# Attention's queries and keys computed channel by token, their rotation and the keys' parts made on GpSimd

## The chip, the cores and the metric

The kernel runs on one core of one Trainium2 chip. The metric is device time of that core in microseconds (us), the median of several runs. A core has TensorE (PE, matrix products and transposes, results in PSUM), VectorE (DVE), ScalarE (ACT), GpSimd (POOL) and SyncE (SP, here the queue that issues most DMAs). Each engine runs its own instructions in the order of the program; semaphores make one wait for another.

## What is computed

One layer of a hybrid block on 512 tokens of width 1024 (in float32). The parts that the change touches are the queries and keys of the attention and the gates of the recurrent branch:

```python
h = rmsnorm(x, norm_g[l])
(a_q, a_k, a_v, a_z, i_q, i_k, i_w,
 b_q, b_k, b_v, b_z, b_o, b_i, b_f, g_a, g_b) = jnp.split(h @ w_in[l], offsets, axis=-1)
q_a = partial_rope(a_q.reshape(Bsz, S, A_HEADS, A_HEAD_DIM), pos)     # 8 heads of 64
k_a = partial_rope(a_k.reshape(Bsz, S, A_HEADS, A_HEAD_DIM), pos)
...
# partial_rope: of 64 channels of a head, 16 are rotated by the token's angle, 48 stay
out = jnp.concatenate([x1 * cos - x2 * sin, x1 * sin + x2 * cos, rest], axis=-1)
...
logits = jnp.einsum('bthd,btjhd->bthj', q_b, k_g) * (Dh ** -0.5)      # per head, chosen keys only
...
# recurrent branch (4 heads of 128): P from running sums and maxima of log_f and log_i
num = w_inter * (qc @ C) + (s_qk @ vc)
```

An indexer (i_q, i_k, i_w) gives each token a score for each earlier key; the best 128 keys take part in its softmax. Both branches are gated, projected, summed, projected once more (w_out), added to x and normalised.

## The kernel before

**Three products for one.** Weights and activations are split into a leading part in fp32r (`w_hi`, `h_hi`) and the remainder (`w_lo`, `h_lo`); the helper `three` (L1483) makes hi·hi, hi·lo and lo·hi, L1486 to L1488. The weights of `w_in` come in slots of 128x1024 (L671): SP loads a slot to `w_raw`, ACT rounds it to `w_hi` (`round_slot`, L875), and POOL subtracts to get `w_lo` (`remainder`, L529). A slot's place is free again when PE has used the slot seven before it.

**Units and places.** PE's work in the first half is a list of units: `small`, then for the groups iq0, iq1 (indexer queries, three units each), aq, ak, bq, bk, bv, av, bo, bz, az four units each. A unit is 24 matmuls of 128x512 into one of two banks `pj`, in four quarters of 6; a quarter is a *place*, and `plan` (L112) puts the small side jobs (transposes, scores, attention heads) behind places by numbers written out by hand. Every engine walks the same list of places and does its part of the side jobs there, in order. With `first["ak"]` as 0, the places of ak are 0 to 15, of bq 16 to 31, of bk 32 to 47, of bv (the recurrent branch's values) 48 to 63, of av (attention's values) 64 to 79. A slot of the next group is rounded, and its remainder made, at the start of each unit, for the last unit of a group at its second place.

**Queries and keys before.** The units aq and ak give token rows (128 tokens x 512 channels). ACT copies the bank to `stage` (L992), DVE rotates 16 channels of each head there (L1138 to L1141, `rotated`), PE transposes the four 128x128 blocks (`stage_chan`, L1541) into a bank `tr`; ACT copies the queries to `q_a` (L904), or rounds the keys to `k_parts` (L913), and DVE subtracts for the keys' remainders (L1259). The indexer's queries go the same way and stay so.

**The recurrent branch at the start of av.** For head h, ACT makes `decay` (L932) and `e_row`, POOL cuts the triangle (`decay_b`, L775, at place 4h of av less 2), PE transposes and multiplies (`kt_b`, `qk_b`, place 4h of av), DVE makes `sp` (L1268, waits for the cut), `q_e` (L1271, both inputs in SBUF), two rounds of the top-k search, and `state` (L1289, L1291), and PE's `pv_b` (L1583, L1586, place 4h+4) waits for `sp`, `q_e` and `state`. POOL's `decay_b` of head 0 stands in its queue behind the remainder of av's fourth slot.

**Gates.** `gate_l` holds 8 columns per token; `gate_rows` (L1529) transposes them in two jobs of four transposes, DVE makes the running rows `a_row` and `nm_row` (L1187 to L1197), and `gate_cols` (L1535) turns these back in eight transposes.

## Time and profile before

| | us |
|---|---|
| median of 3 runs | 505.19 (505.15 to 505.41) |
| the profiled execution | 505.35 |
| its span from first to last instruction | 503.6 |
| PE busy | 494.5 (98%) |
| DVE busy | 261.4 (52%) |
| ACT busy | 239.2 (47%) |
| POOL busy | 213.0 (42%) |

The profile is of one execution. Its page gives busy time by engine, the span in 40 slices, the chain of work that ended last, and groups of instructions; the trace behind it gives each instruction's start and length, and what its engine was waiting for just before. Matmuls are pipelined: a 128x512 matmul is listed with 0.39 us, but the next starts 0.23 us after it, and start to start is what a matmul costs.

### The profile page before, as it was taken

What the parts mean: (1) busy time and instruction counts of PE and PEld (TensorE: products, weight loads), DVE (VectorE), ACT (ScalarE), POOL (GpSimd) and SP (SyncE); (2) the same over time, 40 slices, a digit from 0 to 9 for tenths busy, and PEclk for the clock granted to TensorE, in tenths of its full rate; (3) what the DMA queues carried; (4) which work ended last, traced back from release to release, by engine and by line L of the source; (5) the groups of instructions that cost most, each with busy time, mean ns of one, the idle gap of its engine ahead of it and who ended that gap; (6) DMA issues with size and microseconds to landing.
All of it is one profiled execution on the core that took longest, in us unless ns stands there. A gap on an engine that the chain in (4) does not pass through costs nothing.

```text
span 503.6 us, 6823 instructions
## 1 busy us (share of the span) xinstructions
PE 494.5 (98%) x2518; PEld 411.6 (82%) x2518; DVE 261.4 (52%) x575; ACT 239.2 (47%) x434; POOL 213.0 (42%) x130
## 2 busy tenths in 40 slices
PE   8999999999999999999999999999999999999995
PEld 7688888888888888888788888888888888887885
DVE  3865777877899936525655567531111011125433
ACT  6757655555554455536568652413330333152322
POOL 0675131333344444247487451246534663373000
PEclk9999999999999999999999999999999999999999
DMA  8654432212343243112223112043234426453111
GB/s 284 188 153 128 126 87 79 84 48 80 83 111 99 85 117 104 52 43 85 57 70 85 43 43 65 20 125 104 62 87 125 126 58 193 126 149 144 42 55 72
DMA packets 44841, 48.94 MB, mean 97 GB/s; under 512 B 4996, under 2 KB 30212, under 8 KB 44808
## 3 DMA queue, kind: packets, MB, share of 16 engines
q1 hardware_dynamic: 43944, 47.65, 32.3%
q10 hardware_dynamic: 864, 0.86, 0.5%
q8 instruction: 20, 0.33, 0.3%
q14 instruction: 13, 0.11, 0.1%
HBM read 46.40 MB, written 2.11 MB: 96 GB/s over the span
## 4 chain that ended last, share of the span: by engine, by line
PE 94%; DMA 2%; SPq 1%; POOL 1%; ACT 1%; DVE 1%; issue 1%; DVEq 0%
PE pj L1486 24%; PE pj L1487 24%; PE pj L1488 24%; DMA w_raw<-in_w_in 2%; PE ob L1617 2%; PE tr L1606 2%; PE qb L1554 2%; PE qb L1553 2%; PE ob L1487 1%; PE qb L1487 1%; PE ob L1488 1%; PE qb L1488 1%; PE ob L1486 1%; PE qb L1486 1%; PE tr L1541 1%; PE qb L1601 1%
## 5 line engine op out<-in xcount | busy, mean ns | idle before, releaser
L529 POOL TENSOR_TENSOR w_lo<-w_raw,w_hi 128x1024 fp32r<-128x1024 f32 x70 | 168.9, 2424 | 156.3 <-ACT w_hi L875 156.0
L1486 PE MATMUL pj<-w_hi,h_hi 128*128 128x512 f32 x272 | 109.6, 403 | 0.0
L1488 PE MATMUL pj<-w_hi,h_lo 128*128 128x512 f32 x272 | 106.5, 392 | 0.0
L1487 PE MATMUL pj<-w_lo,h_hi 128*128 128x512 f32 x272 | 106.4, 391 | 0.0
L1486 PE MATMUL pj<-h_hi,w_hi 128*128 128x512 f32 (+1 forms) x200 | 78.1, 390 | 1.0 <-DVE h_lo L1129 1.0
L875 ACT ACTIVATE w_hi<-w_raw 128x1024 fp32r<-128x1024 f32 (+1 forms) x72 | 73.5, 1045 | 9.8 <-DMA w_raw<-in_w_out 6.3
L1488 PE MATMUL pj<-h_hi,w_lo 128*128 128x512 f32 (+1 forms) x200 | 77.9, 389 | 0.0
L1487 PE MATMUL pj<-h_lo,w_hi 128*128 128x512 f32 (+1 forms) x200 | 77.8, 389 | 0.0
L1488 PEld LDWEIGHTS pj<-w_hi,h_lo 128*128 128x128 f32 x272 | 51.1, 188 | 11.4
L1486 PEld LDWEIGHTS pj<-w_hi,h_hi 128*128 128x128 f32 x272 | 51.2, 188 | 8.3 <-issue 0.2
L1487 PEld LDWEIGHTS pj<-w_lo,h_hi 128*128 128x128 f32 x272 | 51.3, 188 | 8.0
L1443 DVE TENSOR_TENSOR prod<-qb,sig 128x512 f32<-128x512 f32 x8 | 5.5, 690 | 77.2 <-PE qb L1488 77.2
L1486 PEld LDWEIGHTS pj<-h_hi,w_hi 128*128 128x128 f32 (+1 forms) x200 | 37.3, 186 | 9.4 <-issue 1.3
L1488 PEld LDWEIGHTS pj<-h_hi,w_lo 128*128 128x128 f32 (+1 forms) x200 | 37.3, 186 | 8.1
L1487 PEld LDWEIGHTS pj<-h_lo,w_hi 128*128 128x128 f32 (+1 forms) x200 | 37.3, 186 | 7.8
L840 POOL TENSOR_TENSOR m_lo<-prod,m_hi 128x512 fp32r<-128x512 f32 x8 | 10.6, 1330 | 60.5 <-ACT m_hi L1088 60.5
L1211 DVE SCALAR_TENSOR_TENSOR score<-ob,idx_w,score 128x512 f32<-128x512 f32 (+2 forms) x45 | 27.7, 616 | 11.5 <-ACT ob L921 8.8
L921 ACT ACTIVATE ob<-qb 128x512 f32<-128x512 f32 (+2 forms) x48 | 22.0, 476 | 16.7 <-PE qb L1554 11.7
L966 ACT ACTIVATE probs<-probs,neg_max 128x128 f32<-128x128 f32 (+3 forms) x32 | 18.0, 562 | 23.3 <-DVE neg_max L1306 23.1
L1088 ACT ACTIVATE m_hi<-prod 128x512 fp32r<-128x512 f32 x8 | 5.1, 632 | 47.3 <-DVE prod L1446 47.3
L1315 DVE COPY probs_t<-tr 128x128 f32<-128x128 f32 (+3 forms) x32 | 15.6, 489 | 22.6 <-PE tr L1606 22.6
L1223 DVE MAX8 top<-score 128x8 f32<-128x512 f32 (+2 forms) x48 | 26.7, 556 | 0.9
(216 smaller groups left out, 817.3 us busy)
## 6 DMA issues: line engine op xcount, KB each, us to landing
w_raw<-in_w_in SPq DMA_DIRECT2D x60, 512.0 KB, 3.6
w_raw<-in_w_out SPq DMA_DIRECT2D x5, 512.0 KB, 3.5
x_tok<-in_x SPq DMA_DIRECT2D x4, 512.0 KB, 5.3
w_raw<-in_w_branch_a SPq DMA_DIRECT2D x8, 256.0 KB, 2.9
w_raw<-in_w_branch_b SPq DMA_DIRECT2D x8, 256.0 KB, 3.3
x_again<-in_x SPq DMA_DIRECT2D x1, 2048.0 KB, 9.3
w_late<-in_w_out SPq DMA_DIRECT2D x3, 512.0 KB, 6.1
out<-y_norm SPq DMA_DIRECT2D x4, 320.0 KB, 2.3
```

The lines of the kernel that those rows point to most:

```text
L529: eng.tensor_tensor(lo[:, 0:m], raw_slot(n)[:, 0:m], hi[:, 0:m].bitcast(F32), ALU.subtract).then_inc(lo_by_dve if n in DVE_SLOTS else lo_b ...
L840: pool.tensor_tensor(m_lo[:, c, :], prod[:, c % 2, 0, :], m_hi[:, c, :].bitcast(F32), ALU.subtract)\
L875: act.activation(split_slot(n)[0][:, 0:m], raw_slot(n)[:, 0:m], ACT.Copy).then_inc(hi_made, 1)
L921: act.activation(ob[s % RELUS][:, 0:w], bank_of(job)[:, 0:w], ACT.Relu, scale=float(IDX_DIM) ** -0.5).then_inc(relu_made, 1)
L966: act.activation(probs[:, s % 2, 0:w], probs[:, s % 2, 0:w], ACT.Exp, scale=-1.0, bias=neg_max[:, s:s + 1], accum_out=p_sum[:, s:s + 1])\
L1211: ins = dve.scalar_tensor_tensor(out=acc, in0=ob[s % RELUS][:, 0:w], scalar=wt, in1=acc, op0=ALU.mult, op1=ALU.add)
L1223: link(dve.max(top8[:, i, :], acc))
L1315: dve.tensor_copy(probs_t[:, s % QUAD, 0:w], bank_of(job)[:, 0:w]).then_inc(probs_t_made, 1)
L1486: pe.matmul(bank, a_hi, b_hi, start=first, stop=False)
L1487: pe.matmul(bank, a_hi, b_lo, start=False, stop=False)
L1488: return pe.matmul(bank, a_lo, b_hi, start=False, stop=last)
L1553: pe.matmul(bank[:, 0:w], queries, ik_hi[:, 0:w], start=True, stop=False)
```

## The change

The units aq and ak are computed channel by token, as bq and bk are: the weights' columns give the rows of the result, so a unit is a block of 128 channels (two heads) over all 512 tokens, and no transpose follows. Rotation now runs across partitions: tables `cos_t` and `sin_t` (made once, from columns that ride in the gates' transpose) hold a factor for each channel row and token; four small DMAs from ACT's queue bring each group's partner rows (8 partitions x 4 x 512 each) into `swapped`, whose other rows are zero; DVE writes result x cos straight from the bank; POOL multiplies `swapped` by `sin_t` and adds it (job `turn`, m 0 to 3 the queries' blocks, 4 to 7 the keys'). The keys' leading parts are made by ACT and their remainders by POOL (job `parts`), in the group bv. The gates' transposes are joined: one `gate_rows` of four transposes 128x128, one `gate_cols` of four 64x64.

```diff
+TURNED = ("aq", "ak")
-STAGED = [u for u in UNITS if u[0] in ("iq0", "iq1", "aq", "ak")]
+STAGED = [u for u in UNITS if u[0] in ("iq0", "iq1")]
+TURNS = [(g, b) for g in TURNED for b in range(KW)]
...
+    for k in range(4):
+        put(first["ak"] + k, "swap", k)
+        put(first["ak"] + 30 + k, "swap", KW + k)
+    for m, p in enumerate((6, 12, 18, 24, 40, 45, 50, 55)):
+        put(first["ak"] + p, "turn", m)
+    for b, p in enumerate((48, 51, 55, 59)):
+        put(first["ak"] + p, "parts", b)
...
+        raw_chan = [at("q_raw", [P, KW, SEQ], F32, z_g2), at("k_raw", [P, KW, SEQ], F32, z_a)]
+        k_chan = at("k_chan", [P, KW, SEQ], F32, z_g2)
...
+            pool.memset(gate_l[:, :, :], 0.0)
+            pool.memset(two_rows[:, :], 0.0)
+            pool.memset(cos_t[:, :], 1.0)
+            pool.memset(sin_t[:, :], 0.0)
+            pool.memset(swapped[:, :, :], 0.0).then_inc(blank_made, 1)
...
+                    if job[0] == "turn":
+                        m = job[1]
+                        g, b = TURNS[m]
+                        pool.wait_ge(rope_made, 4)
+                        pool.wait_ge(swap_in, 64 * (TURNED.index(g) + 1))
+                        pool.tensor_tensor(swapped[:, b, :], swapped[:, b, :], sin_t[:, :], ALU.mult).then_inc(sin_made, 1)
+                        pool.wait_ge(sin_made, m + 1)
+                        pool.wait_ge(cos_made, m + 1)
+                        part = swapped[:, b, :].rearrange("p (t n) -> p t n", n=P)
+                        pool.tensor_tensor(turned_rows(g, b), turned_rows(g, b), part, ALU.add).then_inc(turned, 1)
+                    if job[0] == "parts":
+                        b = job[1]
...
+                        for e in range(2):
+                            src, hi, lo = k_part(b, e)
+                            pool.wait_ge(k_hi_made, 2 * b + e + 1)
+                            pool.tensor_tensor(lo, src, hi.bitcast(F32), ALU.subtract).then_inc(k_lo_made, 1)
+                            pool.wait_ge(k_lo_made, 2 * b + e + 1)
...
+                elif kind == "gate_rows":
...
+                    for first, dst in ((64, cos_t), (96, sin_t)):
+                        for rows in (slice(0, ROT), slice(A_DIM, A_DIM + ROT)):
+                            act.activation(dst[rows, :], bank_of(job)[first:first + ROT, :], ACT.Copy)\
+                                .then_inc(rope_made, 1)
+                elif kind == "swap":
...
+                    act.dma_start(swapped[to:to + HALF, :, :], raw_chan[n][src:src + HALF, :, :]).then_inc(swap_in, 16)
+                elif kind == "parts":
...
+                    act.wait_ge(turned, KW + b + 1)
+                    for e in range(2):
+                        src, hi, _ = k_part(b, e)
+                        act.activation(hi, src, ACT.Copy).then_inc(k_hi_made, 1)
...
-                elif g in ("iq0", "iq1", "aq", "ak"):
+                elif g in TURNED:
+                    act.activation(raw_chan[TURNED.index(g)][:, j, :], src[:, :], ACT.Copy).then_inc(done, 1)
...
+                if g in TURNED:
+                    if g == "ak" and j == 0:
+                        dve.wait_ge(swap_in, 64)
...
+                    dve.tensor_tensor(turned_rows(g, j), pj[u % 2][:, :].rearrange("p (t n) -> p t n", n=P),
+                                      cos_t[:, :].rearrange("p (t n) -> p t n", n=P), ALU.mult).then_inc(cos_made, 1)
...
-                    c = job[1] * B_HEADS
                     for j in range(TILES):
-                        ins = pe.transpose(bank[0:B_HEADS, j * P:(j + 1) * P], gate_l[:, j, c:c + B_HEADS], ident[:, :])
+                        ins = pe.transpose(bank[:, j * P:(j + 1) * P], gate_l[:, j, :], ident[:, :])
...
-                        if g in CHAN_GROUPS:
+                        if g in CHAN_GROUPS + TURNED:
                             a, b = w_part(n, c + j * P, c + (j + 1) * P), h_part(k, 0, SEQ)
```

The numbers of the lines move: `remainder` is L552 in the changed kernel, the decay's cut L826, `sp` L1341, `q_e` L1344, `state` L1362 and L1364, the three products L1567 to L1569.

On PE, at the third place of ak's third unit, before:

```order
444 L1486 MATMUL pj<-w_hi,h_hi 128x512
445 L1487 MATMUL pj<-w_lo,h_hi 128x512
446 L1488 MATMUL pj<-w_hi,h_lo 128x512
447 L1486 MATMUL pj<-w_hi,h_hi 128x512
448 L1487 MATMUL pj<-w_lo,h_hi 128x512
449 L1488 MATMUL pj<-w_hi,h_lo 128x512
450 L1541 MATMUL tr<-ident,stage 128x128 x4
451 L1553 MATMUL qb<-ik_hi,iq_parts 128x256
452 L1554 MATMUL qb<-ik_lo,iq_parts 128x256
```

And the same place after:

```order
441 L1567 MATMUL pj<-h_hi,w_hi 128x512
442 L1568 MATMUL pj<-h_lo,w_hi 128x512
443 L1569 MATMUL pj<-h_hi,w_lo 128x512
444 L1631 MATMUL qb<-ik_hi,iq_parts 128x256
445 L1632 MATMUL qb<-ik_lo,iq_parts 128x256
```

Four transposes are gone, the two operands of each product have changed sides, and the six matmuls of the place and the indexer's score stay as they are. This is so at all eight units of aq and ak.

On POOL, from the top-k part of the program (`v_b`'s ones) to the second cut of `decay`, before:

```order
16 L823 MEMSET v_b 128x16
17 L529 TENSOR_TENSOR w_lo<-w_raw,w_hi 128x1024 x11
18 L775 AFFINE_SELECT decay<-decay 128x512
19 L529 TENSOR_TENSOR w_lo<-w_raw,w_hi 128x1024
20 L775 AFFINE_SELECT decay<-decay 128x512
```

And after, from the last w_lo of bv's slots (the second w_lo of row 38 is av's first slot, rows 43, 47 and 49 its second, third and fourth):

```order
38 L552 TENSOR_TENSOR w_lo<-w_raw,w_hi 128x1024 x2
39 L819 TENSOR_TENSOR k_parts<-k_chan,k_parts 64x512 x2
40 L806 TENSOR_TENSOR swapped<-swapped,sin_t 128x512
41 L810 TENSOR_TENSOR k_chan<-k_chan,swapped 128x512
42 L819 TENSOR_TENSOR k_parts<-k_chan,k_parts 64x512 x2
43 L552 TENSOR_TENSOR w_lo<-w_raw,w_hi 128x1024
44 L806 TENSOR_TENSOR swapped<-swapped,sin_t 128x512
45 L810 TENSOR_TENSOR k_chan<-k_chan,swapped 128x512
46 L819 TENSOR_TENSOR k_parts<-k_chan,k_parts 64x512 x2
47 L552 TENSOR_TENSOR w_lo<-w_raw,w_hi 128x1024
48 L819 TENSOR_TENSOR k_parts<-k_chan,k_parts 64x512 x2
49 L552 TENSOR_TENSOR w_lo<-w_raw,w_hi 128x1024
```

Behind row 49 stand the cut for head 0, the w_lo of bo's first slot and the cut for head 1. Twelve operations have moved in between av's first slot and the cut for head 0; four more (turns 4 and 5) stand just ahead of row 38.

## Rows read from the trace of the kernel before

**Rows 1.** The page: busy time by engine, share of the span, instructions.

```profile
PE 494.5 (98%) x2518; PEld 411.6 (82%) x2518; DVE 261.4 (52%) x575; ACT 239.2 (47%) x434; POOL 213.0 (42%) x130
```

**Rows 2.** Timeline of PE in ak: start, length, instruction.

```profile
119.58 0.60 PE L1541 MATMUL tr<-ident,stage 128*128 128x128 f32 x4
...
120.25 0.39 PE L1487 MATMUL pj<-w_lo,h_hi 128*128 128x512 f32 x1
120.48 0.40 PE L1488 MATMUL pj<-w_hi,h_lo 128*128 128x512 f32 x1
```

**Rows 3.** Timeline of PE around the gates' transposes (gate_rows, then gate_cols).

```profile
33.09 1.03 PE L1529 MATMUL tr<-ident,gate_l 128*4 128x128 f32 x8
...
34.19 0.39 PE L1487 MATMUL pj<-w_lo,h_hi 128*128 128x512 f32 x1
...
44.20 0.40 PE L1488 MATMUL pj<-w_hi,h_lo 128*128 128x512 f32 x1
...
45.45 0.39 PE L1487 MATMUL pj<-w_lo,h_hi 128*128 128x512 f32 x1
```

**Rows 4.** DMA issues: target, size, median us to landing.

```profile
ident<-const_ident ACTq DMA_DIRECT2D x1, 64.0 KB, 4.0
```

**Rows 5.** Timeline of ACT and PE: ak's first unit emptied, a score in the second.

```profile
100.40 0.60 ACT L992 ACTIVATE stage<-pj 128x512 f32<-128x512 f32 x1 [0.75 <-PE pj L1488]
...
107.33 0.28 PE L1553 MATMUL qb<-ik_hi,iq_parts 128*128 128x256 f32 x1
```

**Rows 6.** Timeline of GpSimd from bk's third unit into av.

```profile
157.07 2.40 POOL L529 TENSOR_TENSOR w_lo<-w_raw,w_hi 128x1024 fp32r<-128x1024 f32 x1 [3.04 <-ACT w_hi L875]
...
167.95 2.40 POOL L529 TENSOR_TENSOR w_lo<-w_raw,w_hi 128x1024 fp32r<-128x1024 f32 x1 [2.81 <-ACT w_hi L875]
...
184.50 2.40 POOL L529 TENSOR_TENSOR w_lo<-w_raw,w_hi 128x1024 fp32r<-128x1024 f32 x1 [3.96 <-ACT w_hi L875]
186.85 0.64 POOL L775 TENSOR_SCALAR_AFFINE_SELECT decay<-decay 128x512 f32<-128x512 f32 x1
189.01 2.39 POOL L529 TENSOR_TENSOR w_lo<-w_raw,w_hi 128x1024 fp32r<-128x1024 f32 x1 [1.52 <-ACT w_hi L875]
```

**Rows 7.** Timeline of GpSimd: pairs of operations of the sizes that are added.

```profile
228.13 2.71 POOL L766 TENSOR_TENSOR q_lo<-q_a,q_twice 64x512 fp32r<-64x512 f32 x2
230.92 2.40 POOL L529 TENSOR_TENSOR w_lo<-w_raw,w_hi 128x1024 fp32r<-128x1024 f32 x1
...
261.29 1.29 POOL L828 TENSOR_TENSOR gated<-gated,norm_b_row 128x512 f32<-128x512 f32 x1
...
263.80 2.40 POOL L529 TENSOR_TENSOR w_lo<-w_raw,w_hi 128x1024 fp32r<-128x1024 f32 x1
```

**Rows 8.** Timeline of PE in av: last place of its first unit, first pv_b.

```profile
193.10 0.48 PE L1486 MATMUL pj<-w_hi,h_hi 128*128 128x512 f32 x1
...
195.96 0.61 PE L1583 MATMUL ob<-v_b,sp 128*128 128x129 f32 x4
```

**Rows 9.** Timeline of DVE at head 0 of the recurrent branch.

```profile
190.03 0.69 DVE L1268 SCALAR_TENSOR_TENSOR sp<-qb,decay 128x512 f32<-128x512 f32 x1 [8.51 <-PE qb L1566]
190.64 1.18 DVE L1271 SCALAR_TENSOR_TENSOR q_e<-qk_b,e_row 128x384 f32<-128x384 f32 x1
...
194.29 0.73 DVE L1291 SCALAR_TENSOR_TENSOR state<-state,chunk_w,ob 128x129 f32<-128x129 f32 x2
```

**Rows 10.** One line by itself: length min/median/max in ns (q_e on DVE).

```profile
L1271 DVE SCALAR_TENSOR_TENSOR q_e<-qk_b,e_row x4: 546/548/1177, 190.6 to 216.7; 128x384 f32<-128x384 f32 x4
```

**Rows 11.** Timeline of GpSimd and of DVE near 30 us.

```profile
25.90 7.13 POOL L529 TENSOR_TENSOR w_lo<-w_raw,w_hi 128x1024 fp32r<-128x1024 f32 x3 [3.15 <-ACT w_hi L875]
...
29.16 1.53 DVE L1177 TENSOR_TENSOR gate_l<-gate_l,gate_t 128x16 f32<-128x16 f32 x1
```

**Rows 12.** Windows after the last matmul: window, PE busy, granted clock, DMA share, GB/s.

```profile
498.40:501.50 3.10, 0.00 (x0) 1.00 0.04 18
502.00:502.50 0.50, 0.00 (x0) 0.50 1.05 401
```

More of the change, by code:

```diff
@@ L122, in plan @@
     put(first["iq0"] + 3, "ik_chan")
-    put(first["iq0"] + 8, "gate_rows", 1)
-    put(first["iq0"] + 8, "gate_rows", 0)
+    put(first["iq0"] + 8, "gate_rows")
     put(first["iq1"] + 3, "gate_cols")
@@ L170 @@
            "score": "q", "qk_b": "q", "qk_a": "q", "pv_b": "o", "pv_a": "o", "kt_b": "tr", "state_b": "o"}
-NOT_PE = ("scales_in", "scales", "decay_b")
+NOT_PE = ("scales_in", "scales", "decay_b", "swap", "turn", "parts")
 def fills():
@@ L421, in hybrid_kernel @@
         en_made = sem("en_made")
+        blank_made = sem("blank_made")
+        rope_made = sem("rope_made")
+        swap_in = sem("swap_in")
+        sin_made = sem("sin_made")
+        cos_made = sem("cos_made")
+        turned = sem("turned")
+        k_hi_made = sem("k_hi_made")
+        k_lo_made = sem("k_lo_made")
         rotated = sem("rotated")
@@ L548, in wait_read @@
             elif kind == "gate_rows":
-                eng.wait_ge(rows_read, 2 - job[1])
+                eng.wait_ge(rows_read, 2)
+                eng.wait_ge(rope_made, 4)
             elif kind == "gate_cols":
@@ L616, in part @@
             src = bank_of(job)[same, :].rearrange("p (b t) -> p b t", t=P)
-            if g == "ak":
-                cols = slice(j * P, (j + 1) * P)
-                return src, k_parts[same, e, :, cols], k_parts[other, e, :, cols]
             b0 = 0 if g == "iq0" else 4
@@ L622, in part, with k_part, turned_rows @@
             return src, iq_parts[same, e, b0:b0 + 4, cols], iq_parts[other, e, b0:b0 + 4, cols]
-        def part_unit(job):
-            return job[1] if job[1] < N_IQ else job[1] - TILES
+        def k_part(b, e):
+            same, other = slice(e * A_DIM, (e + 1) * A_DIM), slice((1 - e) * A_DIM, (2 - e) * A_DIM)
+            return k_chan[same, b, :], k_parts[same, e, b, :], k_parts[other, e, b, :]
+        def turned_rows(g, b):
+            return (q_a[:, :, b, :] if g == "aq" else k_chan[:, b, :].rearrange("p (t n) -> p t n", n=P))
         def unit_slots(u):
@@ L706, in _ @@
                     sp.wait_ge(neg_m_kept, 16)
+                    wait_full(sp, ("gate_cols",))
                     for h in range(B_HEADS):
@@ L769, in side @@
                 for job in SIDE.get(p, []):
+                    if job[0] == "turn":
[10 more added lines that the diff above has]
+                        b = job[1]
+                        ready = max(unit_slots(v)[-1] for v in range(p // 4 + 1) if unit_slots(v))
+                        pool.wait_ge(lo_by_pool, sum(1 for m in range(ready + 1) if m not in DVE_SLOTS))
+                        pool.wait_ge(turned, sum(1 for v in SIDE for j in SIDE[v] if j[0] == "turn" and v <= p))
+                        for e in range(2):
[3 more added lines that the diff above has]
+                            pool.wait_ge(k_lo_made, 2 * b + e + 1)
                     if job[0] == "decay_b":
@@ L1006, in evacuate @@
                 elif g == "av":
+                    if j == 0:
+                        act.wait_ge(turned, len(TURNS))
                     act.activation(v_a[:, j, :], src[:, :], ACT.Copy).then_inc(done, 1)
@@ L1021, in split_queries @@
                     wait_full(act, ("qk_a", A_HEADS * (i - 1) - 1))
-                act.wait_ge(q_a_turned, i + 1)
+                act.wait_ge(turned, KW)
                 for e in range(2):
@@ L1254, in job_side @@
                         .then_inc(ik_lo_made, 1)
[L1255 removed]
+                elif kind == "stage_chan":
                     for e in range(2):
                         src, hi, lo = part(job, e)
[L1258 removed]
+                        dve.wait_ge(part_hi_made, 2 * job[1] + e + 1)
                         dve.tensor_tensor(lo, src, hi.bitcast(F32), ALU.subtract).then_inc(part_lo_made, 1)
```

87 lines of the change are left out of this document (47 added, 40 removed).

## Prediction, made before the changed kernel ran

> **What bounds the kernel now.** I read the busy time by engine first: PE is busy 98% of the span, no other engine over half [rows 1]. In a kernel packed like this PE gives back every instruction taken from it, and loses every moment that it is made to wait. So two questions decide: what leaves PE, and whether anything added elsewhere arrives later than PE wants it. For the second I read the timelines of GpSimd, ACT and DVE beside PE's in the stretches where the change puts work, and look at what each engine has queued there. GpSimd looks idle enough on the whole (42%, rows 1), but most of its part of the change is packed into bv, 96 matmuls or 22 us long.
>
> **What PE gives back.** A batch of four transposes starts at 119.58, the second matmul behind it at 120.25; at 0.23 us from start to start [rows 2] that matmul would have started 0.23 us after 119.58, so a batch costs 0.67 - 0.23 = 0.44 us. Eight batches go: 3.52 us. The gates: eight transposes start at 33.09 and L1487 behind them at 34.19, so they cost 1.10 - 0.23 = 0.87; four should cost the 0.44 of rows 2, which saves 0.43. At gate_cols L1488 starts at 44.20 and the second matmul behind it at 45.45, so the eight cost 1.25 - 0.46 = 0.79 [rows 3]; four cost at most 0.44, which saves 0.35 or a little more, say 0.39. Turning the operands' sides costs nothing: the number of 128x512 matmuls is the same, and bq and bk run in that order already. Together 3.52 + 0.43 + 0.39 = **4.34 us**. All of it lies before bq.
>
> **Edits that I cost at nothing.** The five memsets stand where GpSimd waits for the first weights to be loaded. ACT's four copies into the tables come where ACT waits for the next transposes, and DVE's product with cos replaces a rotation of about the same length. The swaps: the fourth of the queries' DMAs is issued only after ACT has emptied ak's first unit (100.40 to 101.0, rows 5), and DVE waits for it before its own first product of ak. A DMA of the same 64 KB from ACT's queue took 4.0 us to land [rows 4]. DVE would be free again near 105.7, finish the score that it owes near 106.2, and ACT would pass on the next near 106.7; the PE score that needs it stood at 107.33 [rows 5], now at 106.9. It just fits: 0, at most some 0.5 if a DMA is slower. The keys' swaps have 10 us to spare.
>
> **GpSimd in bv, step by step.** I keep the times of before; up to here PE has moved by 4.34 and everything that it paces with it. The w_lo at 157.07 [rows 6] ends at 159.45 and turns 4 and 5 follow. A turn is two 128x512 operations; the pair at 261.29 is over at 263.80 [rows 7], 2.51 us. Two turns end at 164.47, the w_lo of bv's fourth slot at 166.85, 2.6 us before PE wants it, and the w_lo of av's first slot starts at 167.95 as before, since it waits for ACT. From there GpSimd never rests again. A pair of remainders 64x512 takes from 228.13 to 230.92, 2.79 us, with the waits on its own semaphore [rows 7]; a w_lo takes 2.38 (7.13 for three, rows 11), a waiting successor adds some 0.09 (to a turn 0.13). So: w_lo 2.47, parts 2.79, turn 2.64, parts 2.79, w_lo 2.38, turn 2.64, parts 2.79, w_lo 2.47, parts 2.79, w_lo 2.35 = 26.11. The cut for head 0 starts at 167.95 + 26.11 = 194.06 instead of 186.85 [rows 6], and av's fourth slot is ready near 194.1, where PE wanted it at 193.10 [rows 8].
>
> That 1 us is not the whole price, because GpSimd's cut is what DVE's sp waits for. The cut takes 0.6: sp starts at 194.7 instead of 190.03 and q_e at 195.35. Here a second thing bites. q_e took 1.18 us at 190.64 [rows 9] and 0.55 in the other three cases [rows 10]. At 190.64 GpSimd was in the w_lo of 189.01 [rows 6], which ended at 191.4, and q_e ended 0.42 after that. The same is seen at 29.16: an operation on 16 columns lasted 1.53 us, until 30.69, and GpSimd's second w_lo from 25.90 ended at about 30.65 [rows 11]. So a DVE operation that reads two SBUF operands stands still until GpSimd's running operation is over. After the change the w_lo of bo's first slot starts right behind the cut, 194.66, and ends at 197.05; q_e ends near 197.47. From q_e's end (191.82) to state's end (195.02) was 3.20 us [rows 9], all DVE's own work; state is now ready at 200.67, and PE's first pv_b starts near 200.72 instead of 195.96 [rows 8]: **4.76 us late**. The wait of 1 us for the slot lies inside this. Head 1 follows at PE's pace, GpSimd catches up in av, and nothing behind it becomes shorter, since PE is full there.
>
> The Trainium skill has a rule for this ("SBUF — State Buffer", section "SBUF: two separate sides"): VectorE and GpSimd share a port pair, and an operation of VectorE with two SBUF inputs is blocked for a whole GpSimd operation that reads SBUF. By that rule, the rows at 190.64 and 29.16 agree (ends 0.42 and 0.04 us after GpSimd's). If contention merely stretched q_e to its 1.18 us, the wait would be 4.0 instead of 4.76.
>
> ACT gains a wait too: the last parts job asks for turn 7, ready at 183.6, where ACT comes by at 182.5. Behind it stand the fourth slot's rounding (then done near 185.9, GpSimd wants it at 191.7) and the decay of head 0 (done by 187.3). This costs nothing.
>
> **Sum.** 505.35 (the profiled execution) - 4.34 + 4.76 = 505.77; the median lies 0.16 below that execution, so **505.6 us**. The gain from the transposes is real and is spent on one wait in av. Ends of the unknown costs: if the twelve operations on GpSimd took 1.19 each, half of a w_lo, the queue would be 2.1 us shorter (503.5); at 1.4 each, 0.4 longer (506.0).
>
> **The rivals.**
> - *The queue is shorter than I make it.* GpSimd gets through some parts faster, or q_e slips in ahead of the w_lo; q_e alone at 0.55 ends at 195.9 and takes 1.56 us off: 504.1. With faster remainders too, down to 503.2. For it: no row shows these very operations. Against: the rows of the same sizes agree among themselves. Chance 0.22; from a wait of 3.3 us down the kernel is faster by over 0.2%.
> - *It is all hidden.* If GpSimd is not behind at the cut, the gain stays whole: 505.19 - 4.34 = 500.85. Against it is the sum of 26 us of work in a stretch of 22. Chance 0.06.
> - *The change costs more than it gives: PE's clock falls.* PE would stand from about 197.1 to 200.7, 3.6 us, with one more wait shortly before. After the last matmul (it started at 498.10) the granted clock was still 1.00 up to 501.5 and 0.50 at 502.0 [rows 12], so an idle stretch only a little longer did bring the lower level, 1.2 GHz. If it falls here, PE runs at half pace for a while; if that lasts as long as the idle stretch did, it loses 1.8 us: 507.4. It decides once the wait in av reaches what the end of the span shows. Chance 0.14. The Trainium skill ("TensorE: Matmul & The Clock Gate", section "Part 1: The HAM clock gate (the "warmup" mystery)") says that an idle array is set back to 1.2 GHz and must first be busy again; by that rule the outcome is this rival's, 507.4, if the stretch counts as idle.
> - *Another new wait.* ak's first product waiting for a swap longer than 4 us, or ACT held by `turned` and late with a rounding; each 1 to 2 us on top: about 506.8. Chance 0.12.
>
> **How the numbers follow.** The forecast has 0.46 and a range of its own from 504.9 to 506.5. A measurement tells about 0.2% (1.0 us) from no change, so same is 504.2 to 506.2. The forecast gives 0.40 to same and 0.06 to slower; the short queue 0.15 to faster and 0.07 to same; all hidden 0.06 to faster; the clock 0.14 and another wait 0.12 to slower. That is 0.21 faster, 0.47 same, 0.32 slower. The range from 503.2 to 507.6 takes in the short queue and the lower clock, and leaves out the hidden case and a pile of several waits.
>
> **What would show it.** PE's timeline: no L1541 in aq and ak, first matmul of bv 4.3 us earlier. GpSimd without a gap from av's first w_lo to the cut, the cut 26.1 us after that w_lo's start. q_e near 2.1 us long, ending 0.4 after a w_lo. PE waiting about 3.6 us in front of the first pv_b and 1 us in front of av's fourth slot; a clock below 1.00 in a window behind it would be the third rival. I am wrong if GpSimd's queue has gaps in bv, if PE's wait names another engine than DVE's state, or if a wait shows in ak.

## The result, and the profile of the changed kernel

| | before | after |
|---|---|---|
| median | 505.3 us (505.15 to 505.57, 4 executions) | 508.33 us (507.65 to 509.1, 4 executions) |
| ratio | 1 | 1.006, 95% interval 1.004 to 1.0079 |
| profiled execution | 505.35, span 503.6 | 508.95, span 507.2 |
| mean granted clock of PE in the profiled execution | 0.998 | 0.992 |

The change makes the kernel slower by 0.6%. That lies above the range of the prediction, by 0.7 us. The four executions of the changed kernel lie in two pairs, 507.65 and 507.71, 508.95 and 509.1; those of the kernel before lie within 0.4 us. This spread turns out to be part of the answer.

The busy time by engine, on the page of the changed kernel, stands beside [rows 1]:

```profile
PE 492.6 (97%) x2478; PEld 409.5 (81%) x2478; DVE 257.0 (51%) x552; ACT 239.8 (47%) x434; POOL 247.5 (49%) x159
```

Forty instructions of PE are gone and 29 have come to GpSimd, with 34.5 us. PE's busy time fell by only 1.9 us, although the forty instructions were worth more than 4: what is left must have become slower somewhere. The waits of PE (engine, line, what it waited for: total, times, longest) name the new ones:

```profile
PE ob L1661 <- DVE state L1364: 3.6, 1, 3.6
...
PE pj L1567 <- POOL w_lo L552: 0.9, 1, 0.9
```

(PE's waits for `x_norm` in the first 12 us are longer too, 2.0 us in all against 0.8. They cost nothing here: the first product starts at 13.40, against 13.51 before.)

The chain to the first of the two new waits is the predicted one. GpSimd's timeline, the w_lo of av's first slot, head 0's cut and the w_lo behind it (answers to [rows 6]):

```profile
163.76 2.40 POOL L552 TENSOR_TENSOR w_lo<-w_raw,w_hi 128x1024 fp32r<-128x1024 f32 x1 [0.86 <-ACT w_hi L926]
...
189.94 0.64 POOL L826 TENSOR_SCALAR_AFFINE_SELECT decay<-decay 128x512 f32<-128x512 f32 x1
190.55 2.41 POOL L552 TENSOR_TENSOR w_lo<-w_raw,w_hi 128x1024 fp32r<-128x1024 f32 x1
```

The first of them is 4.19 us earlier than before: PE's gain is there. From it to the cut GpSimd has no gap for 26.18 us. DVE's timeline (answers to [rows 9]):

```profile
190.72 0.69 DVE L1341 SCALAR_TENSOR_TENSOR sp<-qb,decay 128x512 f32<-128x512 f32 x1 [13.37 <-POOL decay L826]
191.33 2.04 DVE L1344 SCALAR_TENSOR_TENSOR q_e<-qk_b,e_row 128x384 f32<-128x384 f32 x1
...
195.84 0.73 DVE L1364 SCALAR_TENSOR_TENSOR state<-state,chunk_w,ob 128x129 f32<-128x129 f32 x2
```

DVE stood for 13.37 us until GpSimd made the cut; q_e then took 2.04 us and ended at 193.37, 0.41 after GpSimd's w_lo; the state is ready at 196.57. PE's timeline (answers to [rows 8]), and what follows:

```profile
190.04 0.50 PE L1567 MATMUL pj<-w_hi,h_hi 128*128 128x512 f32 x1 [0.88 <-POOL w_lo L552]
...
196.68 1.20 PE L1661 MATMUL ob<-v_b,sp 128*128 128x129 f32 x4 [3.63 <-DVE state L1364]
...
200.88 0.63 PE L1568 MATMUL pj<-w_lo,h_hi 128*128 128x512 f32 x1
201.31 0.63 PE L1569 MATMUL pj<-w_hi,h_lo 128*128 128x512 f32 x1
...
202.83 0.38 PE L1661 MATMUL ob<-v_b,sp 128*128 128x129 f32 x2
```

The first pv_b took 1.20 us for what took 0.61 before [rows 8], and two neighbouring matmuls of the projection start 0.43 us apart, where 0.23 is the rule [rows 2]. The windows over this stretch (window, its length, busy time of PE, PEld, DVE, ACT and POOL, PE's granted clock, DMA share, GB/s) say why:

```profile
193.00:195.50 2.50, 0.06 (x1) 0.00 (x0) 2.38 (x7) 0.28 (x1) 2.50 (x2) 1.00 0.59 155
195.50:196.60 1.10, 0.00 (x0) 0.00 (x0) 0.99 (x3) 0.00 (x0) 0.68 (x1) 0.62 0.35 132
196.60:202.40 5.80, 5.72 (x22) 5.36 (x23) 1.67 (x4) 1.27 (x4) 0.00 (x0) 0.50 0.31 90
202.40:204.00 1.60, 1.60 (x12) 1.42 (x12) 1.49 (x5) 0.08 (x1) 0.00 (x0) 0.94 0.00 0
```

While PE waits, its clock falls from 2.4 to 1.2 GHz (at about 195.75, by the share of 0.62), and it is back only at about 202.6. PE works 5.9 us of that time, at half pace. From the first pv_b to the second one of head 0 took 6.15 us (196.68 to 202.83); in the profile before the same work took 3.28 (195.96 [rows 8] to 199.24):

```profile
199.24 0.38 PE L1583 MATMUL ob<-v_b,sp 128*128 128x129 f32 x2
```

So 2.87 us are lost there.

The account of the spans: up to the values' group PE gained 4.26 (the first pv_b would stand at 191.70, as the first experiment shows), the waits of PE ahead of the first pv_b cost 4.98 (196.68), the low clock 2.87: together +3.59 of the measured +3.6. (In the experiments with a stop and a full clock the same work takes 3.34 to 3.39 instead of 3.28, so up to 0.1 of the 2.87 belongs to the start after a stop.) My theory for the experiments was this account. The rivals: the gain of the transposes is smaller and the loss diffuse; the matmuls behind the stop are slow for another reason than the stop.

### The profile page after: what moved, and what is told of

Its sections match the earlier page's. It is cut to its first block, busy times and chain, and to the rows that moved or that the text cites. A ratio compares the mean times of both kernels' runs of the same rounds, so it can differ in the third digit from the quotient of the medians.

```text
span 507.2 us, 6774 instructions
## 1 busy us (share of the span) xinstructions
PE 492.6 (97%) x2478; PEld 409.5 (81%) x2478; DVE 257.0 (51%) x552; ACT 239.8 (47%) x434; POOL 247.5 (49%) x159
## 4 chain that ended last, share of the span: by engine, by line
PE 59%; POOL 2%; DVE 2%; issue 1%; ACT 0%; DVEq 0%; POOLq 0%
PE pj L1567 14%; PE pj L1568 14%; PE pj L1569 14%; PE ob L1695 2%; PE tr L1684 2%; PE ob L1568 1%; PE ob L1567 1%; PE qb L1568 1%; PE qb L1567 1%; PE ob L1569 1%; PE qb L1569 1%; POOL k_parts L819 1%; POOL w_lo L552 1%; PE qb L1679 1%; PE ob L1661 1%; PE qb L1678 1%
## 5 line engine op out<-in xcount | busy, mean ns | idle before, releaser
L552 POOL TENSOR_TENSOR w_lo<-w_raw,w_hi 128x1024 fp32r<-128x1024 f32 x70 | 169.3, 2430 | 121.6 <-ACT w_hi L926 121.2
L1567 PE MATMUL pj<-h_hi,w_hi 128*128 128x512 f32 (+1 forms) x264 | 103.1, 391 | 1.0 <-DVE h_lo L1203 1.0
L1568 PE MATMUL pj<-h_lo,w_hi 128*128 128x512 f32 (+1 forms) x264 | 103.0, 390 | 0.0
L1569 PE MATMUL pj<-h_hi,w_lo 128*128 128x512 f32 (+1 forms) x264 | 102.9, 390 | 0.0
L1567 PE MATMUL pj<-w_hi,h_hi 128*128 128x512 f32 x208 | 85.0, 409 | 0.9 <-POOL w_lo L552 0.9
L1568 PE MATMUL pj<-w_lo,h_hi 128*128 128x512 f32 x208 | 81.7, 393 | 0.0
L1569 PE MATMUL pj<-w_hi,h_lo 128*128 128x512 f32 x208 | 81.7, 393 | 0.0
L1567 PEld LDWEIGHTS pj<-h_hi,w_hi 128*128 128x128 f32 (+1 forms) x264 | 49.3, 187 | 11.1 <-issue 1.2
L1569 PEld LDWEIGHTS pj<-h_hi,w_lo 128*128 128x128 f32 (+1 forms) x264 | 49.3, 187 | 10.9
L1568 PEld LDWEIGHTS pj<-h_lo,w_hi 128*128 128x128 f32 (+1 forms) x264 | 49.3, 187 | 9.4
L1569 PEld LDWEIGHTS pj<-w_hi,h_lo 128*128 128x128 f32 x208 | 39.3, 189 | 8.8
L1567 PEld LDWEIGHTS pj<-w_hi,h_hi 128*128 128x128 f32 x208 | 39.4, 190 | 7.8 <-POOL w_lo L552 1.1
```

The costliest lines, as they stand in the source:

```text
L552: eng.tensor_tensor(lo[:, 0:m], raw_slot(n)[:, 0:m], hi[:, 0:m].bitcast(F32), ALU.subtract).then_inc(lo_by_dve if n in DVE_SLOTS else lo_b ...
L1567: pe.matmul(bank, a_hi, b_hi, start=first, stop=False)
L1568: pe.matmul(bank, a_hi, b_lo, start=False, stop=False)
L1569: return pe.matmul(bank, a_lo, b_hi, start=False, stop=last)
```

## The experiments

A ratio is the time of a kernel divided by that of the kernel before, which ran beside it: at 505.19 us beside the early cut, the remainders on DVE, the work for PE and q_e ahead of the cut; at 505.21 beside the stops put in by hand; at 505.31 beside the place alone, the transposes put back and the changed kernel once more.

### Head 0's cut put earlier

```
-    for b, p in enumerate((48, 51, 55, 59)):
+    for b, p in enumerate((48, 51, 55, 63)):
...
-        put(p - 2, "decay_b", h)
+        put(p - (6 if h == 0 else 2), "decay_b", h)
```

> The changed kernel with two jobs moved in the values' group: the decay of head 0 (ScalarE's exponentials and GpSimd's cut) is put four quarters earlier, ahead of the keys' fourth parts, and the fourth parts four quarters later. Nothing is left out. Theory (GpSimd's queue makes the cut of head 0 late, TensorE stops for 3.6 us, and its clock then stands at 1.2 GHz for some 5.8 us): the cut ends before 188, neither the stop nor the low clock appears, granted clock back to 0.998, and the time is 508.3 - 4.5 - 2.9 = 501 us. Rival (the 3.6 us that the changed kernel lost are spread over other places, or the shorter transposes never gave 4.2 us at the end): 504 to 506 us. Rival (the keys' fourth parts, now later, make the first cell copy of ScalarE wait, and a new stop comes): 503 to 505 us.

Measured: 501.24 us (501.06 to 501.39), ratio 0.992, interval 0.9907 to 0.9934; clock 0.998. GpSimd's and PE's timelines of this kernel:

```profile
184.71 0.65 POOL L826 TENSOR_SCALAR_AFFINE_SELECT decay<-decay 128x512 f32<-128x512 f32 x1
...
187.81 2.86 POOL L819 TENSOR_TENSOR k_parts<-k_chan,k_parts 64x512 fp32r<-64x512 f32 x2
...
191.70 0.61 PE L1661 MATMUL ob<-v_b,sp 128*128 128x129 f32 x4
```

The cut is made 5.2 us earlier, the first pv_b starts without a wait at 191.70, that is 4.26 before [rows 8], and PE's waits hold nothing of the values' groups any more. Two numbers of the order table give back 7.1 us of the median of 508.33 (6.5 of the 507.7 that the last experiment measured for the changed kernel). This kernel, called the quiet kernel from here on, holds every part of the change and is 0.8% faster than the kernel before and 1.3 to 1.4% faster than the changed one. So the same work on the same engines can be had without the loss, and what costs is the order in GpSimd's queue. Two jobs were moved, the cut of 0.64 us and the keys' fourth parts; the next experiment moves only the cut.

### The place alone

```
-        put(p - 2, "decay_b", h)
+        put(p - (6 if h == 0 else 2), "decay_b", h)
...
+                        pool.wait_ge(decay_cut, h + 1)
```

> The changed kernel with head 0's decay and cut put four quarters earlier and the keys' fourth parts left where they are, ahead of GpSimd's remainder of the last quarter of the attention's values. Nothing is left out. It tells whether the place of the cut or the length of GpSimd's queue is what costs. Theory: the cut is made at about 185, so VectorE's state is in time; but the queue is as long as before, and that remainder ends at about 190.7 where TensorE wants it at 189.1: a stop of 1.5 us there, too short to bring the clock down: 501.24 + 1.5 = 502.7 us. Rival (only the place of the cut matters): 501.2 us. Rival (the clock falls even so): 504.4 us.

Measured: 503.06 us (503.02 to 503.63), ratio 0.9958, interval 0.9946 to 0.9971; clock 0.999. PE's waits, and GpSimd's timeline:

```profile
PE pj L1568 <- POOL w_lo L552: 1.7, 1, 1.7
```

```profile
184.56 0.65 POOL L826 TENSOR_SCALAR_AFFINE_SELECT decay<-decay 128x512 f32<-128x512 f32 x1
185.29 2.87 POOL L819 TENSOR_TENSOR k_parts<-k_chan,k_parts 64x512 fp32r<-64x512 f32 x2
188.24 4.71 POOL L552 TENSOR_TENSOR w_lo<-w_raw,w_hi 128x1024 fp32r<-128x1024 f32 x2
```

(The added line makes GpSimd wait for its own cut before it goes on.) The wait is 1.7 us where 1.5 was expected, and the time is 501.24 + 1.8. So both hold: the place of the cut decides about most of the loss, and the queue's length about the rest. The clock stayed up in all five executions (0.997 or more) behind this stop of 1.7 us.

### The keys' remainders on DVE

```
                 elif kind == "parts":
...
+                        dve.wait_ge(k_hi_made, 2 * b + e + 1)
+                        dve.tensor_tensor(lo, src, hi.bitcast(F32), ALU.subtract).then_inc(k_lo_made, 1)
```

(taken out of GpSimd's program)

> The changed kernel with one part of the change undone: the eight remainders of the keys' parts are made by VectorE, which in the changed kernel stands idle for 13.37 us before the decayed scores of head 0; GpSimd keeps the rotation. Nothing is left out. Theory: GpSimd's queue in the values' group is 4 x 2.7 = 10.7 us shorter, the cut of head 0 follows ScalarE's exponentials at about 186, no stop of TensorE, no low clock: 501 us. Rival (the rotation alone already makes the queue too long, or VectorE's remainders in the top-k rounds push these back into the next stage): a stop of 1 to 2 us stays, 502.5 to 505 us.

Measured: 503.54 us (503.5 to 503.96), ratio 0.9968, interval 0.9956 to 0.9981. The theory's number was wrong here and the rival's range holds it. PE's waits, GpSimd's and DVE's timelines:

```profile
PE ob L1662 <- issue: 1.8, 1, 1.8
```

```profile
183.12 1.11 POOL L821 TENSOR_SCALAR_AFFINE_SELECT decay<-decay 128x512 f32<-128x512 f32 x1
```

```profile
182.43 2.33 DVE L1333 TENSOR_TENSOR k_parts<-k_chan,k_parts 64x512 fp32r<-64x512 f32 x2
...
189.27 0.69 DVE L1342 SCALAR_TENSOR_TENSOR sp<-qb,decay 128x512 f32<-128x512 f32 x1
...
192.90 0.73 DVE L1365 SCALAR_TENSOR_TENSOR state<-state,chunk_w,ob 128x129 f32<-128x129 f32 x2
```

GpSimd now makes the cut at 183.12, so its queue is cured. But sp stands at 189.27, and not for the cut: DVE has no idle time ahead of it. The four pairs (this one 2.33 us, others up to 3.37) push the top-k rounds between them back by some 11 us. Of the 13.37 us that DVE stood idle in the changed kernel only 8.5 were free; the rest was the wait for the cut (in the kernel with the early cut sp starts at 185.77, when PE's product is there). The state is 1.8 us late instead of 3.6. That wait is named "issue" in the profile, though it ends with DVE's state at 193.63: the label of a wait needs the other engine's timeline beside it. PE's clock was 1.00 throughout.

### The clock: work for PE during the wait

```
+                    if (h, g) == (0, 0):
+                        for _ in range(14):
+                            pe.matmul(bank[:, :], h_hi[:, 0, 0:P], h_hi[:, 0, :], start=True, stop=True)
                     wait_read(pe, ("qk_b", h))
```

> The changed kernel with 14 extra products of 128x512 on TensorE just ahead of the products of head 0's cells, into their bank, which is overwritten afterwards: the result is not touched, and the wait for VectorE stays as long as it was, but TensorE works through most of it (14 x 0.23 = 3.2 of the 3.6 us). Theory (the second half of the loss is TensorE's clock, which falls because the engine stands idle): granted clock 1.00 to the end of the stage, and 508.3 - 2.9 = 505.4 us (504.8 to 506). Rival (the matmuls after the stop are slow for another reason, such as contention with GpSimd and VectorE in the on-chip memory, or the stop does not matter to the clock): 508 to 509 us.

Measured: 506.2 us (505.97 to 506.43, 11 executions), ratio 1.0019, interval 1.001 to 1.0028; clock 0.998. PE's timeline and the windows:

```profile
192.96 3.33 PE L1658 MATMUL ob<-h_hi 128*128 128x512 f32 x14
196.74 0.68 PE L1664 MATMUL ob<-v_b,sp 128*128 128x129 f32 x4 [0.45 <-issue]
```

```profile
193.00:196.70 3.70, 3.29 (x15) 2.40 (x13) 3.43 (x10) 0.34 (x1) 3.30 (x3) 1.00 0.49 148
196.70:202.40 5.70, 5.66 (x38) 5.18 (x39) 3.17 (x8) 2.42 (x9) 0.00 (x0) 1.00 0.30 92
```

The first pv_b starts at 196.74, 0.06 later than in the changed kernel: DVE and GpSimd are exactly as late as there. Yet the clock stays at 1.00 and PE gets 38 matmuls done between 196.7 and 202.4, where it got 22 done in nearly the same stretch of the changed kernel. The span is 504.5 instead of 507.2: 2.7 us come back by pure extra work. My 505.4 was 0.8 too low, since I took the full 2.9 off the median of 508.33, in which the low clock costs less than in the profiled execution; by the spans, 507.2 - 2.87 + 0.06 = 504.4, it fits. What this kernel is slower than the one before, 0.9 by the spans, is mostly the wait less the gain: its first pv_b stands at 196.74 instead of 195.96.

### q_e ahead of the cut

```
-                    dve.wait_ge(decay_cut, h + 1)
...
-                    dve.scalar_tensor_tensor(out=sp[:, h % 2, :], in0=bank_of(job)[:, :], scalar=float(B_DIM) ** -0.5,
...
                     dve.wait_ge(e_row_made, h + 1)
                     dve.scalar_tensor_tensor(out=q_e[:, h % 2, :], in0=qk_b[:, h, P:SEQ], scalar=float(B_DIM) ** -0.5,
...
+                    dve.wait_ge(decay_cut, h + 1)
+                    dve.scalar_tensor_tensor(out=sp[:, h % 2, :], in0=bank_of(job)[:, :], scalar=float(B_DIM) ** -0.5,
...
```

> The changed kernel with two operations of VectorE swapped for every head: q_e, which needs no cut, is made ahead of the wait for the cut, sp behind it. Nothing is left out. For head 0 q_e then lies in VectorE's idle time and out of reach of GpSimd's remainder, beside which it took 2.04 us instead of 0.55. Theory: the state is ready 2.0 us earlier, the stop shrinks from 3.6 to 1.6 us. If a stop of 1.6 us leaves the clock at 2.4 GHz: 508.3 - 2.0 - 2.9 = 503.4 us. If the clock falls after it just the same: 506.3 us. Rival (q_e was not on the path, the copies of the state wait for something else): 508.3 us.

Measured: 504.32 us (504.14 to 504.86, 11 executions), ratio 0.9984, interval 0.9975 to 0.9993. DVE's and PE's timelines:

```profile
185.96 0.75 DVE L1341 SCALAR_TENSOR_TENSOR q_e<-qk_b,e_row 128x384 f32<-128x384 f32 x1 [8.50 <-PE qb L1644]
190.93 0.69 DVE L1344 SCALAR_TENSOR_TENSOR sp<-qb,decay 128x512 f32<-128x512 f32 x1 [4.21 <-POOL decay L826]
...
194.09 0.73 DVE L1364 SCALAR_TENSOR_TENSOR state<-state,chunk_w,ob 128x129 f32<-128x129 f32 x2
```

```profile
194.92 0.69 PE L1661 MATMUL ob<-v_b,sp 128*128 128x129 f32 x4 [1.54 <-issue]
```

q_e took 0.75 us, the stop shrank from 3.63 to 1.54, and the clock stayed up in all eleven executions. From the start of sp to the end of the state are 3.89 us (190.93 to 194.82) instead of 5.85 (190.72 to 196.57): q_e beside GpSimd's w_lo was on the path, with 1.96 of its 2.04 us. The first pv_b stands only 1.8 us earlier (194.92 against 196.68), since the wait for av's fourth slot grew from 0.9 to 1.1. So the change of order on an otherwise idle engine is worth 1.8 us in the wait and about as much again or more in the clock: 4.0 together by the median of 508.33, 4.5 by the spans. The expected 503.4 is 0.9 too low for the reason given above: it took the full 2.9 off that median.

The Trainium skill ("SBUF — State Buffer", section "SBUF: two separate sides") has a GpSimd operation that reads SBUF and an operation of VectorE with two SBUF inputs exclude each other for a whole instruction; the 2.04 us in the changed kernel, ending 0.41 behind GpSimd's w_lo, agree.

### The stop put in by hand

The quiet kernel of the first experiment, with ScalarE making copies for which PE waits ahead of the first pv_b (3, 5 and 9 of them):

```
+                        for m in range(3):
+                            act.activation(v_a[:, 1, :], neg_m_all[:, 0, :], ACT.Copy).then_inc(held, 1)
+                            act.wait_ge(held, m + 1)
...
+                        pe.wait_ge(held, 3)
```

> The kernel of e1_cut_early (501.24 us, no stop) with a stop put in by hand: ScalarE makes 3 copies of 128x512 one behind the other, into a place that it overwrites later, after the values' first batch, and TensorE waits for the last of them ahead of head 0's cells. ScalarE is free some 0.36 us after TensorE's last product, and a copy with its hand-over is taken as 0.66 us, so the stop is about 2.3 us. If a stop of this length leaves the clock at 2.4 GHz: 501.2 + 2.3 = 503.5 us. If the clock falls: 503.5 + 2 to 3 = 505.5 to 506.5 us.

> As e5_hold3 with 5 copies: a stop of about 3.7 us, as long as that of the changed kernel, with GpSimd, VectorE and the order of all else as in the quiet kernel. Theory (the stop alone brings the clock down, and that costs 2 to 3 us): 501.2 + 3.7 + 2.1 to 2.9 = 507 to 507.8 us, with some 6 us at 1.2 GHz behind the stop. Rival (the low clock of the changed kernel comes from something else there): 504.9 us and granted clock 1.00.

> As e5_hold3 with 9 copies: a stop of about 6.3 us. Theory (the price of the low clock is that of the work behind the stop and does not grow with the stop): 501.2 + 6.3 + 2.1 to 2.9 = 509.6 to 510.4 us. Rival (the stretch at 1.2 GHz begins at a fixed time after the stop began and is over that much sooner, so a longer stop hides part of it): 501.2 + 6.3 + 0.5 to 1.5 = 508 to 509 us. Rival (it grows with the stop): 511 us or more.

The last one is the kernel before the change with the five copies and nothing else:

> The kernel before the change with the same stop by hand, 5 copies of ScalarE, about 3.7 us at the same place, and nothing of the change in it. Theory: the clock falls here too, 505.2 + 3.7 + 2.1 to 2.9 = 511 to 511.8 us. Rival (the fall needs something of the changed kernel, such as GpSimd's longer queue): 508.9 us.

Measured, with the stop in us as PE's waits show it in the profiled execution:

| kernel | stop | median | executions |
|---|---|---|---|
| quiet, 3 copies | 2.1 | 505.03 | 4 at 503.4 to 503.6, 8 at 504.8 to 505.4 |
| quiet, 5 copies | 3.4 | 506.57 | 2 at 504.7 to 504.9, 5 at 506.2 to 506.6, 4 at 507.2 to 508.0 |
| quiet, 9 copies | 6.1 | 509.53 | 4 at 508.9 to 510.1 |
| before, 5 copies | 3.4 | 510.53 | 1 at 509.05, 3 at 510.4 to 510.7 |

The mean granted clock goes with the steps: with 5 copies it is 0.998 in the two lowest, 0.994 to 0.996 in the middle five, 0.992 in the highest four. The lowest step is each time the stop alone (501.24 + 2.1 = 503.3; 501.24 + 3.4 = 504.6; 505.2 + 3.4 = 508.6, the measured ones lie 0.1 to 0.4 above), the next lies about 1.6 above it, the last 2.4 to 3.2. So for the same kernel the fall comes in some executions and not in others; for the executions that were not profiled this is read from their time and their mean granted clock. None of the four medians lies in the range that I gave for a fallen clock: each is 0.1 to 0.5 us below it, because the theory let the clock fall in every execution and at the full price. The profile of the kernel with 3 copies caught an execution where it fell, PE's timeline and the windows:

```profile
193.91 0.71 PE L1668 MATMUL ob<-v_b,sp 128*128 128x129 f32 x4 [2.09 <-ACT v_a L1029]
...
198.88 0.38 PE L1668 MATMUL ob<-v_b,sp 128*128 128x129 f32 x2
```

```profile
194.00:195.00 1.00, 1.00 (x9) 1.00 (x10) 0.00 (x0) 0.07 (x1) 1.00 (x1) 1.00 0.79 147
195.00:196.00 1.00, 1.00 (x8) 1.00 (x7) 0.00 (x0) 1.00 (x4) 0.95 (x1) 0.56 0.96 367
196.00:198.00 2.00, 2.00 (x8) 1.71 (x8) 1.15 (x3) 0.10 (x1) 0.00 (x0) 0.50 0.44 91
198.00:199.00 1.00, 1.00 (x6) 0.83 (x5) 0.96 (x4) 0.00 (x0) 0.00 (x0) 0.73 0.90 346
```

PE had been at work again since 193.91 when the clock fell at about 195.1, and it stayed low for 3.4 us. From the first pv_b to the second took 4.97 us, 1.6 more than the 3.38 with 5 copies and a full clock (below); half of 3.4 is 1.7. With 5 copies the profile caught an execution in which it did not fall at all, after a longer stop:

```profile
195.35 0.71 PE L1668 MATMUL ob<-v_b,sp 128*128 128x129 f32 x4 [3.42 <-ACT v_a L1029]
...
198.73 0.38 PE L1668 MATMUL ob<-v_b,sp 128*128 128x129 f32 x2
```

```profile
195.30:202.40 7.10, 7.05 (x47) 6.40 (x48) 3.59 (x10) 3.60 (x12) 1.45 (x2) 1.00 0.39 124
```

With 9 copies the fall comes within the stop, at about 194.1, and the low clock lasts until 201.0 (PE's timeline, then the windows):

```profile
198.05 1.23 PE L1668 MATMUL ob<-v_b,sp 128*128 128x129 f32 x4 [6.06 <-ACT v_a L1029]
...
202.81 0.38 PE L1668 MATMUL ob<-v_b,sp 128*128 128x129 f32 x2
```

```profile
194.00:195.00 1.00, 0.00 (x0) 0.00 (x0) 0.00 (x0) 0.94 (x3) 1.00 (x1) 0.57 0.67 96
195.00:198.00 3.00, 0.00 (x0) 0.00 (x0) 0.00 (x0) 2.87 (x5) 1.11 (x1) 0.50 0.62 180
198.00:200.00 2.00, 1.95 (x9) 1.95 (x10) 0.00 (x0) 0.21 (x1) 0.00 (x0) 0.50 0.53 206
200.00:201.00 1.00, 1.00 (x7) 1.00 (x6) 0.00 (x0) 0.80 (x4) 0.00 (x0) 0.52 0.00 0
```

That is 6.8 us, of which PE works 2.9 (from 198.05): the first pv_b to the second took 4.76, a loss of 1.4 to 1.5. So in these profiles the price is half of what remains of the low stretch once PE works again, and in this one the longer stop hid more of it. The first rival of that run (the loss shrinks) is right for this execution; the four together, 508.9 to 510.1, lie across both ranges, so between these two the medians do not decide. The kernel before the change with 5 copies shows the same steps (its profile, too, caught the one execution in which the clock stayed up; the other three lie 1.3 to 1.7 us higher at a mean clock of 0.994 to 0.995). So the stop is enough, and nothing else of the change is needed.

### The transposes put back

In the quiet kernel, in the third quarter of the unit behind each unit of the queries and keys:

```
+                    if q == 2 and UNITS[u - 1] in TURNS:
+                        wait_read(pe, ("stage_chan", len(STAGED) - 2))
+                        for b in range(4):
+                            pe.transpose(bank_of(("stage_chan", len(STAGED) - 2))[:, b * P:(b + 1) * P], ident[:, :],
+                                         ident[:, :])
```

> The quiet kernel e1_cut_early (501.24 us) with eight batches of four 128x128 transposes put back on TensorE, at the quarters where the kernel before the change had those of the queries and keys, their output unused. Theory: each batch costs what it cost in the trace of before, 0.44 us, and nothing hides it: 501.24 + 3.52 = 504.8 us. Rival (most of the 4 us that TensorE's path became shorter came from elsewhere, such as fewer waits in the queries' and keys' groups): 501.5 to 503.5 us.

Measured: 504.76 us (504.63 to 505.46, 11 executions), 3.52 above the quiet kernel, the very number that was worked out. That it meets it to the last digit is luck: each measured against the kernel before that ran beside it, the difference is 3.40, and in the profiles the first pv_b stands 3.6 us later (195.28 against 191.70). A batch thus costs 0.43 to 0.45 us. For the gates, four transposes of gate_l[:, j, 0:4] and four of two_rows[0:4] are put ahead of those that are there (the expectation says 8, the edit and the trace have 4):

> The quiet kernel e1_cut_early (501.24 us) with the gates' transposes that the change saved put back: four of 128x8 ahead of the gates' rows, four of 8x128 ahead of the gates' columns, their output unused or overwritten. Theory: 0.43 + 0.39 = 0.82 us, 502.06 us. Rival (the small transposes are hidden, since TensorE waits for the gates' rows anyway): 501.2 us.

Measured: 502.21 us (501.85 to 502.58), 0.97 above the quiet kernel (0.85 against the kernels before beside them), where 0.82 was expected. The two together make 4.49, or 4.25; the quiet kernel is 3.95 faster than before by the medians and 4.2 by the spans. So the price of a batch is settled, and the sum is right within some 0.3 to 0.5 us, which the runs do not divide further. The gates' transposes alone start anywhere from 32.78 to 33.11 in the profiles, although PE's instructions ahead of them are the same.

### The changed kernel once more

> The changed kernel once more, for the spread of its executions: the four so far lie at 507.7 (two) and 509.0 (two). Theory (TensorE's clock falls behind the stop in nearly every execution, for one stretch of about 3.4 us, which costs 1.6, or for one of twice that, which costs 2.9): all at 506.1, 507.7 or 509.0 us, few at the first. Rival (the difference is noise of the chip, spread evenly): between 507 and 509.5 us without steps.

Measured: 507.7 us (507.57 to 508.56, 5 executions), ratio 1.0049, interval 1.0035 to 1.0063. The profiled execution is the one of 508.56. PE's timeline, and the windows:

```profile
196.50 1.20 PE L1661 MATMUL ob<-v_b,sp 128*128 128x129 f32 x4 [3.62 <-DVE state L1364]
```

```profile
194.00:195.00 1.00, 0.00 (x0) 0.00 (x0) 0.93 (x4) 0.00 (x0) 1.00 (x1) 1.00 0.86 203
195.00:196.00 1.00, 0.00 (x0) 0.00 (x0) 0.93 (x3) 0.00 (x0) 1.00 (x1) 0.50 0.76 295
...
200.00:201.00 1.00, 1.00 (x5) 0.90 (x4) 0.49 (x1) 0.00 (x0) 0.00 (x0) 0.50 0.00 0
201.00:202.00 1.00, 1.00 (x4) 0.77 (x4) 1.00 (x3) 0.00 (x0) 0.00 (x0) 0.59 0.00 0
```

The same 3.62 us of stop, and 6.8 us of low clock again, but from 195.0 instead of 195.75: 5.3 us of it are left behind the stop, and the second pv_b starts at 202.37, 5.87 behind the first: 2.6 lost, 0.3 less than in the first profile, and this execution is 0.4 faster. Of the nine executions of this kernel five lie at 507.57 to 507.71 and four at 508.14 to 509.1; none lies at the 506.1 that a full clock would give. My steps of 507.7 and 509.0 were too neat: the upper group is spread by when the fall comes. The median of all nine is 507.71, so the 508.33 of the first four is on the high side. That the lower group has one stretch of 3.4 us is inferred from the steps of the kernels with copies; none of its executions was profiled.

## Why the prediction was wrong, point by point

- **What bounds the kernel, and the gain of PE: right.** 4.34 us were worked out, 4.26 stand at the first pv_b of the quiet kernel, and eight batches put back cost 3.4 to 3.6 where the sum has 3.52.
- **The edits costed at nothing: right.** In ak DVE waits for the fourth swap, in its timeline of the changed kernel:

```profile
101.22 0.69 DVE L1437 TENSOR_TENSOR k_chan<-pj,cos_t 128x512 f32<-128x512 f32 x1 [1.59 <-DMA swapped<-q_raw]
```

  PE has no wait there, and none for the tables or for ScalarE. The forecast called this place just fitting, with 0.2 us to spare; there were 1.8. DVE's product starts 2.6 us after ACT has emptied ak's first unit, where the 4.0 of the other DMA was reckoned; ACT's next copy of a score is over at 102.77, and the PE score that needs it stands at 104.53.
- **GpSimd in bv: right.** 26.11 us from av's first w_lo to the cut were worked out from rows of other operations, 26.18 were measured. So close a match is partly luck: each pair of remainders took about 0.05 less than reckoned, each turn 0.16 more. The wait for av's fourth slot is 0.9 (I said 1).
- **q_e held by GpSimd: right.** 2.04 us measured, "near 2.1" said; the run with q_e ahead of the cut took it out and the state was ready 1.96 us sooner after sp began.
- **The wait in front of the first pv_b: right in kind, 0.2 short.** 4.98 against 4.76, in small pieces: 0.07 because av's first w_lo stood 4.19 and not 4.26 earlier, 0.07 in the queue, 0.14 from the cut to sp, 0.06 from the state to pv_b, less 0.12 up to q_e's end. With it the sum would have been 505.35 - 4.26 + 4.98 = 506.07, and 506.2 is what the kernel with a kept-up clock measured. Had the clock not fallen, the result would have been in the range.
- **The clock: the step that failed.** In the sum the low clock stood at nothing; it cost 2.87 us in the profiled execution. I had it only as the third rival, with 0.14 and 1.8 us. *The chance:* the rival's own condition was that the wait "reaches what the end of the span shows", an idle stretch from 498.10 with the fall after 501.5 [rows 12]; the forecast itself put PE's stop at 3.6 us with another wait shortly before. So the forecast met the condition of its rival, and I priced it as an exception. Nor was that stretch a threshold: a stop of 2.1 us brought the clock down in 8 of 12 executions, one of 3.4 in 9 of 11 (and in 3 of 4 of the kernel before), and this kernel's 3.63 in nine of nine, by their times and mean clocks. (This kernel also has the wait of 0.9 us shortly before, which those with copies have not; whether it adds to the fall was not tested.) *The price:* I let the low clock last as long as the stop. In the profiles it lasted 6.8 us behind stops of 3.6, 3.6 and 6.1 us and 3.4 behind one of 2.1, and it began late in the stop or behind it; in the profiled execution 5.9 us of it met work, 2.87 lost. With 1.6 to 2.9 on 506.1 the time is 507.7 to 509.0, which is what was measured. For the lower of the two groups of executions my 1.8 was about right, by luck and not by its reason; for the upper it was up to 1.1 short.
- **The range and the chances.** The upper end 507.6 was just above that rival's 507.4; with the measured prices it would have been 509. The other rivals did not come: no short queue, nothing hidden, no new wait in ak.

Of the page of the Trainium skill that the prediction cited ("TensorE: Matmul & The Clock Gate", section "Part 1: The HAM clock gate (the "warmup" mystery)"), the trace agrees with both halves: the idle PE was set back to 1.2 GHz, and it worked 5.9 us before it had 2.4 GHz again. The page also says that the moment at which the clock rises differs from run to run. Here the fall differs as well: with 3 copies one program took 503.4 to 505.4 us, and in some of its executions the mean clock shows no fall.

## What to carry to other kernels

An idle engine with a queue in order is not free capacity: look at what will stand behind the added work in that queue, above all short operations that others wait for, and put those first. On a kernel in which PE is busy nearly all the time, price a stop of PE like those seen here (2.1 us or more) as the stop and half of the low clock behind it, here 1.4 to 2.9 us, and not as a rare case. Where a stop can't be avoided, shortening it (here to 1.8 us or less), or letting PE work through it, gives back much of the clock's price too: 2.7 us of the span with PE at work through the stop.
